# Attention units of a transformer mixing stage: projections moved around the transposes, small vector work moved in its queue

## What is computed

```python
h = rmsnorm(x, norm_mix)
z = h @ w_in                                # all projections of the layer
o_a = nsa_mixer(...)        # 4 heads: compressed, selected, window attention, gated
o_b = diff_mixer(...)       # 4 heads: softmax(q0 k0) - lam * softmax(q1 k1)
o_c = mlstm_mixer(...)      # causal convolution, gates, decayed scores
o_d = dilated_mixer(...)    # 3 dilated patterns
x = x + concat(o_a, o_b, o_c, o_d) @ w_out
h = rmsnorm(x, norm_ffn)
x = x + (silu(h @ w_gate) * (h @ w_up)) @ w_down
```

## Time and profile before

| | us |
|---|---|
| median of three executions | 2076.34 |
| profiled execution, its own time | 2077.95 |
| its span in the profile | 2076.2 |
| TensorE matmul busy | 1702.6 |
| VectorE busy | 706.7 |
| ScalarE busy | 359.4 |
| chain of waits, share on TensorE matmuls | 48% |

### The profile page before, as it was taken

The page is one execution under the profiler, slowest core; times in us unless marked ns, Lnnn a source line. Parts: engine busy times, 40 slices in busy tenths (PEclk is TensorE's granted clock), DMA queues, the critical chain, the costliest instruction groups (busy, mean ns, idle before and its releaser), DMA issues.

```text
span 2076.2 us, 31931 instructions
## 1 busy us (share of the span) xinstructions
PE 1702.6 (82%) x14144; PEld 1154.0 (56%) x14144; DVE 706.7 (34%) x1255; ACT 359.4 (17%) x832; POOL 79.9 (4%) x85
## 2 busy tenths in 40 slices
PE   6999889969978585556555688989999889899997
PEld 3665458848962251122111256657994466659963
DVE  2005473362340410000000024464664243546663
ACT  2010213232321220000000022421010124310000
POOL 0000004203300000000000000000000000000000
PEclk7999999978998797788778898989999989899999
DMA  9431120000004959999999961213545522134450
GB/s 375 180 122 41 65 82 3 3 1 3 4 3 182 397 245 427 428 427 428 428 428 428 427 230 47 102 56 116 209 169 197 194 101 82 41 122 168 175 196 21
DMA packets 35164, 381.57 MB, mean 184 GB/s; under 512 B 6674, under 2 KB 10130, under 8 KB 12242
## 3 DMA queue, kind: packets, MB, share of 16 engines
q1 hardware_dynamic: 35028, 379.53, 45.7%
HBM read 378.46 MB, written 1.05 MB: 183 GB/s over the span
## 4 chain that ended last, share of the span: by engine, by line
PE 48%; DMA 11%; DVE 4%; ACT 2%; issue 1%; SPq 0%; DVEq 0%; ACTq 0%
PE psum L2619 14%; PE psum L1764 7%; PE psum L2690 7%; DMA arena<-in_w_moe 6%; PE psum L2055 5%; DMA weight_ring<-in_w_moe 5%; PE psum L2058 3%; PE psum L2210 3%; PE psum L1726 3%; PE psum L2186 1%; PE psum L2165 1%; PE psum L1706 1%; PE psum L2074 0%; ACT arena L2262 0%; PE psum L2151 0%
## 5 line engine op out<-in xcount | busy, mean ns | idle before, releaser
L1764 PE MATMUL psum<-weight_ring,arena 128*32 128x512 f32 x640 | 142.6, 716 | 126.5 <-DMA arena<-in_w_moe 92.2
L1188 PE MATMUL psum<-arena 64*64 64x64 f32 x4608 | 151.4, 223 | 20.3 <-PEq L945 8.2
L2619 PE MATMUL psum<-arena 128*128 128x128 f32 x1408 | 165.2, 275 | 1.7 <-DVE arena L2822 1.7
L2619 PEld LDWEIGHTS psum<-arena 128*128 128x128 f32 x1408 | 161.1, 192 | 2.0 <-issue 2.0
L1188 PEld LDWEIGHTS psum<-arena 64*64 64x64 f32 x4608 | 143.7, 138 | 28.2 <-issue 24.2
L1764 PEld LDWEIGHTS psum<-weight_ring,arena 128*32 128x32 f32 x640 | 35.9, 129 | 204.9 <-issue 204.9
L1899 DVE COPY arena<-psum 128x512 f32<-128x512 f32 x16 | 11.1, 692 | 370.3 <-PE psum L1764 370.3
L2619 PE MATMUL psum<-arena,weight_ring 128*128 128x128 f32 x1056 | 131.9, 283 | 4.7 <-ACT arena L2736 2.6
L1764 PE MATMUL psum<-arena 128*32 128x512 f32 x384 | 107.4, 726 | 34.3 <-DMA weight_ring<-in_w_moe 33.9
L2619 PEld LDWEIGHTS psum<-arena,weight_ring 128*128 128x128 f32 x1056 | 127.3, 199 | 5.9 <-DVE arena L2867 3.1
L2055 PE MATMUL psum<-arena,weight_ring 128*128 128x256 f32 x512 | 123.8, 401 | 0.0
(11 more groups left out here) (491 smaller groups left out, 2250.1 us busy)
## 6 DMA issues: line engine op xcount, KB each, us to landing
weight_ring<-in_w_moe SPq DMA_DIRECT2D x60, 2048.0 KB, 20.2
arena<-in_w_moe SPq DMA_DIRECT2D x36, 2048.0 KB, 20.2
weight_ring<-in_w_in SPq DMA_DIRECT2D x23, 2048.0 KB, 8.4
weight_ring<-in_w_mod SPq DMA_DIRECT2D x12, 2048.0 KB, 8.7
weight_ring<-in_w_gate SPq DMA_DIRECT2D x12, 2048.0 KB, 8.0
weight_ring<-in_w_up SPq DMA_DIRECT2D x12, 2048.0 KB, 7.6
weight_ring<-in_w_down SPq DMA_DIRECT2D x12, 2048.0 KB, 7.6
weight_ring<-in_w_out SPq DMA_DIRECT2D x6, 2048.0 KB, 8.0
```

The source lines that it names most:

```text
L1188: last = nc.tensor.matmul(K.ps[half[d], bank, column + HD * n:column + HD * n + HD], lhs(d, h), rhs(d, h), start=True, stop=True, skip_gro ...
L1764: last = nc.tensor.matmul(K.ps[strip(j), 4, :], xsT[:, k, CAP * e:CAP * e + CAP], ws[j][:, k, :], start=(k == 0), stop=(k == KT - 1), skip ...
L2619: last = nc.tensor.matmul(K.ps[:, bank, P * n:P * n + P], lhs, rhs, start=(n == 0 and k == 0 and name in ("m1", "m5", "m6")), stop=(k == 3 ...
```

## The change

The order of the items changes on TensorE and ScalarE, and four pieces of VectorE and ScalarE work change places. No arithmetic is added or left out.

1. `j7` is issued behind `score(0)` instead of ahead of it.
2. In units 0 to 3 one whole projection (`j8`, `j10`, `j12`, `j14`) is issued between `score(u+1)` and `turn(u)`; before, the unit's projections all came behind `turn(u)`. In unit 3, `aq` comes behind `j14` and `turn(3)`, where it came ahead of `j14`.
3. In units 4 to 10 the unit's projection (`j15` to `j21`) is cut into two halves of four contraction steps: one ahead of `turn(u)`, one behind it. The other items (`ks`, `mq0`, ...) come behind the second half. In unit 4, `ks` comes behind `j15`, where it came ahead.
4. On ScalarE, the exponentials of the lambdas and of the forget gates follow `j1`'s copy instead of those of all first items. `item(j)` of a leading projection comes ahead of `keep(u)`; that of a halved one behind `exps(u+1)`.
5. On VectorE, `forget_gates` and `nlam` come ahead of the rotations of `bq` and `bk`; `convolve` moves from unit 0 to unit 3.

```diff
-    before_units = ["j0", "j1", "j2", "j3", "j4", "bq", "j5", "j6", "bk", "j7"]
-    fills = [["j8", "j9"], ["j10", "j11"], ["j12", "j13", "cmp"], ["aq", "j14"], ["ks", "j15"], ["j16", "mq0"], ["j17", "mq1"],
-             ["j18", "f"], ["j19", "dq"], ["j20", "dk", "qk0"], ["j21", "qk1"], ["o0"], [], []]
+    before_units = ["j0", "j1", "j2", "j3", "j4", "bq", "j5", "j6", "bk"]
+    first_fill = "j7"
+    leads = {0: "j8", 1: "j10", 2: "j12", 3: "j14"}
+    halved = {4: "j15", 5: "j16", 6: "j17", 7: "j18", 8: "j19", 9: "j20", 10: "j21"}
+    fills = [["j9"], ["j11"], ["j13", "cmp"], ["aq"], ["ks"], ["mq0"], ["mq1"], ["f"], ["dq"], ["dk", "qk0"], ["qk1"], ["o0"],
+             [], []]
...
+        def half_job(name, i):
+            if i == 0:
+                await_bank(name)
+            last = job(int(name[1:]), banks[at[name]][0], range(4 * i, 4 * i + 4))
+            if i == 1:
+                last.then_inc(made, 1)
...
         score(0)
+        item(first_fill)
         for u in range(NU):
             if u + 1 < NU:
                 score(u + 1)
+            if u in leads:
+                item(leads[u])
+            if u in halved:
+                half_job(halved[u], 0)
             turn(u)
+            if u in halved:
+                half_job(halved[u], 1)
             for name in fills[u]:
                 item(name)
             values(u)
...
-        for name in before_units:
+        for name in before_units[:2]:
             item(name)
         act.wait_ge(lam_ready, once)
         nc.scalar.activation(lsum, lsum, ACT.Exp).then_inc(lam_exp, 1)
         act.wait_ge(f_abs, once)
         nc.scalar.activation(fa, fa, ACT.Exp, scale=-1.0).then_inc(f_exp, 1)
+        for name in before_units[2:]:
+            item(name)
         exps(0)
+        item(first_fill)
         for u in range(NU):
+            if u in leads:
+                item(leads[u])
             keep(u)
             if u + 1 < NU:
                 exps(u + 1)
+            if u in halved:
+                item(halved[u])
...
         lambdas()
-        rotate("bq")
-        rotate("bk")
         forget_gates()
         dve.wait_ge(lam_exp, once)
         link(nc.vector.tensor_tensor(nlam, lsum[:, 1:2], lsum[:, 0:1], ALU.subtract))
         link(nc.vector.tensor_scalar(nlam, nlam, -lam_init, None, ALU.add))
+        rotate("bq")
+        rotate("bk")
         maxima(0)
...
-            if u == 0:
-                convolve()
             if u == 1:
                 cut_blocks()
+            if u == 3:
+                convolve()
```

More of the change, by code:

```diff
@@ L1968, in mixing @@
     NU = len(units)
-    before_units = ["j0", "j1", "j2", "j3", "j4", "bq", "j5", "j6", "bk", "j7"]
-    fills = [["j8", "j9"], ["j10", "j11"], ["j12", "j13", "cmp"], ["aq", "j14"], ["ks", "j15"], ["j16", "mq0"], ["j17", "mq1"],
-             ["j18", "f"], ["j19", "dq"], ["j20", "dk", "qk0"], ["j21", "qk1"], ["o0"], [], []]
+    before_units = ["j0", "j1", "j2", "j3", "j4", "bq", "j5", "j6", "bk"]
[4 more added lines that the diff above has]
+             [], []]
+    around = lambda u: [leads[u]] if u in leads else [halved[u]] if u in halved else []
     after_units = ["o3", "o1", "o2"]
     (x_in, x_at), place_free = K.x_ready, K.place_free
-    items = before_units + [name for fill in fills for name in fill] + after_units
+    items = before_units + [first_fill] + [name for u, fill in enumerate(fills) for name in around(u) + fill] + after_units
     at = {name: n for n, name in enumerate(items)}
@@ L2040, in turn_input, with job @@
                 last.then_inc(t_made, 1)
-        def job(n, bank):
+        def job(n, bank, ks):
             s, kind, b, width, dst = jobs[n]
@@ L2047, in job @@
             w = slot[1]
-            for k in range(KT):
+            for k in ks:
                 if n == 0 and k == 4:
@@ L2062, in job, with await_bank @@
             return last
+        def await_bank(name):
+            for m in held[at[name]]:
+                pe.wait_ge(took[by(items[m])], ordinal[m])
+        def half_job(name, i):
[4 more added lines that the diff above has]
+                last.then_inc(made, 1)
         def item(name):
             n = at[name]
-            for m in held[n]:
-                pe.wait_ge(took[by(items[m])], ordinal[m])
+            await_bank(name)
             bank = banks[n][0]
             if name[0] == "j":
-                last = job(int(name[1:]), bank)
+                last = job(int(name[1:]), bank, range(KT))
             elif name in turns:
```

## The result

The changed kernel takes 2057.71 us (median of 4 executions, 2052.31 to 2061.85), the kernel before 2079.88 (4 executions beside them, 2073.32 to 2089.35). The ratio is 0.9888, 95% interval 0.9841 to 0.9936: 22 us or 1.1% faster. I had forecast 2054.5, in a range of 2046 to 2066. The profiled execution took 2057.97 us, with a span of 2056.2 against 2076.2, so the profiles differ by 20.0 us.

The account below looks back on a forecast made before the run. TensorE's work plus holes released by VectorE bounds the stage. Gains of 13.6 (second layer) and 13.2 us (first), together 26.8, less 4 for clock falls, give 22.8 us and a forecast of 2054.5, range 2046 to 2066.

Parts of the forecast that it names:

- my own sign of 11 to 13.5 us in each stretch: Sign of being right: each layer's attention stretch gets 11 to 13.5 us shorter.
- Start: `bk` to `turn(0)`, second layer: 3.5 us of idle, net of a new 2.1 us wait, plus 3.4 of clock: 6.9.
- The fall behind it: Clock falls behind the new 2.1 us wait ahead of `score(0)`, costing 2.0 us a layer, 4 in all.
- The rival in which the clock stays up: No clock fall at the new wait ahead of `score(0)`: 26.8 us won, 2050 us; chance 0.26.
- Unit 2: At `turn(2)`, 5.0 us of cover for a 5.1 us chain; 6.3 us won in the second layer.
- the clock part of the 6.2: Clock share of the gain around `turn(2)`: 2.3 us on two projections, besides 0.45 on `turn(2)`.
- Units 4 to 9: Half projections cover holes at `turn(6)` and `turn(9)`, 1.6 us; new 1.1 us wait ahead of `score(6)`; net +0.4 a layer.
- Costed at nothing: Moved exponentials, `convolve`, the copy of `j8` and the cutting of projections: 0 us; cuts at most 0.1 us each.
- The slower rival: Transposes between half projections keep TensorE at half clock, units 4 to 10: about 2105 us; chance 0.04.

Follow-up runs that it names:

- e2: Changed kernel with `j7` again ahead of `score(0)`, `j8` behind it and `j9` halved around `turn(0)`; 2050.2 us, 0.9863 of the kernel before.
- e1: Changed kernel with `ks` in unit 4 issued between `score(5)` and the first half of `j15`; 2057.3 us, 0.9898 of the kernel before.
- e4: Changed kernel with TensorE's new order kept and the small VectorE and ScalarE moves undone; 2054.5 us, 0.9884 of the kernel before.
- e6: Changed kernel with units 3 to 10 in the order of before, projections whole; 2060.3 us, 0.9905 of the kernel before.
- e7: Changed kernel with `j12` again behind `turn(2)`; 2061.0 us, 0.9917 of the kernel before.
- e9: e8 with ScalarE copying `j16` ahead of `exps(6)` in unit 5; 2032.8 us, 0.9797 of the kernel before.
- e5: Kernel before with its own order of projections and only the small moves made; 2074.8 us, 0.9979 of the kernel before.
- e3: Changed kernel with the edits of e1 and e2 together; 2055.5 us, 0.9885 of the kernel before.
- e8: e3 with `j21` moved whole from unit 10 to unit 12, between `turn(12)` and `values(12)`; 2037.4 us, 0.9808 of the kernel before.
- e10: e8 unaltered, run a second time; 2048.7 us, 0.9856 of the kernel before.
- e11: e3 unaltered, run a second time; 2048.2 us, 0.9856 of the kernel before.

## Why the prediction was right, and which term was not

From the starts of the same instructions in both timelines: in the second layer `bk`, `values(0)`, the compression, `qk0` and the output product's transposes start at 1674.31, 1696.42, 1720.78, 1782.54 and 1813.79 us before, and at 1664.53, 1681.55, 1699.72, 1763.00 and 1794.25 after. Second layer, first layer in brackets:

| stretch | forecast gain | measured |
|---|---|---|
| `bk` to `values(0)` | 6.9 less 2.0 of clock = 4.9 (4.6) | 5.1 (4.7) |
| `values(0)` to the compression | 6.3 (6.2) | 6.2 (6.0) |
| compression to `qk0` | +0.4 | -1.5 (-1.5) |
| `qk0` to the output product | 0 | 0.0 (0.7) |
| sum | 11.6 (11.2) | 9.8 (9.8) |

The other parts of the span moved by 0.5 us or less each. The 0.7 us of the first layer's last stretch is clock, which I had at nothing: `turn(13)` took 1.30 us, 1.97 before.

The total came out closer than the mechanism deserves. The forecast of 22.8 us stands against 22.2 between the medians, but against 19.6 in the two attention stretches, where all of it was to come from, and my own sign of 11 to 13.5 us in each stretch failed (9.8 and 9.8). What is missing is missing in units 4 to 9, 1.9 us a layer, and small gains elsewhere hide a part of it.

*Start.* Right in mechanism and size: the wait ahead of `score(0)` was forecast at 2.1 and is 2.11, VectorE's rotation releases it, `turn(0)` finds its data. The fall behind it was priced at 2.0; the projection took 5.41 against 3.73 for the projection at the same place in e2, 1.7 us. The rival in which the clock stays up failed in both layers and both profiles. But my ground for the fall was weaker than I made it. The row at 1636.04 has a second wait right behind it (TensorE's timeline, kernel before, second layer):

```profile
1636.04 1.09 PE L2039 MATMUL psum<-arena 128*128 128x128 f32 x8 [2.14 <-DVE arena L2475]
1638.41 6.70 PE L2058 MATMUL psum<-weight_ring,arena 128*128 128x512 f32 x8 [1.28 <-DVE arena L2479]
```

The eight transposes between the two waits took 1.09 us, which is full rate; only the work behind the second wait was slow. The nearest row with one wait alone is the hole of 2.52 us, behind which the clock did fall. So no row of before showed what one wait of 2.1 us does, and choosing the fall was in part luck. The Trainium skill's section that sets the limit for idle gaps above this wait ("TensorE: Matmul & The Clock Gate", "Why this matters for your kernels") does not describe this kernel: behind 2.11 us of waiting the clock fell in all twelve cases (both layers of the two profiles of the changed kernel and of e1, e4, e6 and e7).

*Unit 2.* Right: 5.1 us of chain against 5.0 of cover, and `turn(2)` starts 0.2 us late. In e7 the hole cost its 3.5 us net again, but the whole loss was 3.3 and 3.5: the clock part of the 6.2 is not a fixed price.

*Units 4 to 9.* The step that failed is "so a new wait of 1.1 us ahead of `score(6)`. Net +0.4". The wait was right (1.24), but I priced it as idle time only. Behind it the clock fell: 3.41 - 2.00 on the half projection and 0.91 - 0.60 on `turn(5)` (the full-clock values are those of e9 and e7), 1.7 us together. 1.6 of holes - 1.24 - 1.7 = -1.4, and -1.5 was measured. I had looked for a fall only at the wait that resembled the known ones, and had called 1.08 us safe from one row. It is not: in e6 the clock fell at 1.09. The price is much the same wherever one wait stands alone: 1.7 us here, at `score(0)`, at `turn(2)` in e7 and behind the new wait in e1.

*Costed at nothing.* e4 shows that the small moves are indeed worth nothing on top of the order, and e5 that they are not nothing without it. The cuts themselves cost next to nothing: six of them lie between the compression and `qk0`, where 0.1 us stands between the sum and the measurement, and unit 7, which has no wait in either kernel, takes 5.05 us before and 5.09 after from `score(8)` to `f`.

*The slower rival.* Clock 1.00 inside the cut units (the row at 1737 us), so transposes between half projections did not hold it down here, against what the Trainium skill's "Part 4: PE-mode transpose" would suggest.

## What to carry to other kernels

Filling a hole on the bound engine paid its length here each time, and its clock price only sometimes; price every wait that an edit adds in both coins, the one-microsecond ones too. Before moving a filler away, ask what it covered where it stood (`j7` the rotation of `bk`, 3.5 us a layer), and before removing a wait, walk the other engines' queues for what is late next: e1 won almost nothing because a copy behind ScalarE's table loads was late next, and e9, which moved that copy ahead, took the wait away. When one part of a program varies by 10 us between executions, compare profiles from a common instruction on, and medians only beside them.

## What the hardware showed that I had not expected

The falls of the clock repeat with the kernel, not with the length of the wait. Two profiles of one kernel had their attention stretches equal within 0.2 us (129.0 and 129.7, then 128.8 and 129.8; 125.7 and 123.7, then 125.8 and 123.8; 122.5 and 125.1 both times). Yet a wait of 1.24 us at the same place, behind the same work, was followed by a fall in the changed kernel and by none in e7, and one of 1.09 by a fall in e6 and by none (1.08) in the kernel before. Even the two layers of one kernel differ: behind 1.06 or 1.07 us ahead of `j17` the clock fell in the second layer of e1 and in the first of e3, e8, e10 and e11, and not in the other layer. What decides is not settled by these runs. That a wait of about 1 us can cost nearly 3 us in all is.
